# Two token groups through the norms of a two-layer transformer step: the last weight units are used twice, latent tokens first and context tokens second, and the layer loops are written out

## What is computed

```python
for l in range(2):
    h = rmsnorm(x, g[0]) * (1 + scale0) + shift0
    x = x + 0.5 * gate0 * rmsnorm(swiglu(h, wg[0], wu[0], wd[0]), g[1])   # 1024 -> 2816 -> 1024
    h = rmsnorm(x, g[2]) * (1 + scale1) + shift1
    x = x + gate1 * rmsnorm(mix(h @ w_in) @ w_out, g[3])    # Fourier | Hyena | attention
    h = rmsnorm(x, g[4]) * (1 + scale2) + shift2
    x = x + 0.5 * gate2 * rmsnorm(swiglu(h, wg[1], wu[1], wd[1]), g[5])
```

## Time and profile before

| | |
|---|---|
| median of 3 runs | 1707.72 us (1707.42 to 1708.83) |
| span of the profiled execution, first to last instruction | 1706.8 us |
| PE busy | 1607.5 us, 94% |
| PEld busy | 1462.8 us, 86% |
| DVE busy | 899.6 us, 53% |
| ACT busy | 765.5 us, 45% |
| mean granted PE clock | 0.985 of 2.4 GHz |
| moved by DMA | 268.20 MB, mean 157 GB/s |

### The profile page before, as it was taken

One profiled execution on the slowest core, in us unless ns is written; L12 is line 12 of the kernel. 1 busy time (PEld: TensorE's weight loads), 2 busy tenths in 40 slices (PEclk: granted clock), 3 DMA queues, 4 the chain that ended last, 5 costly groups with the idle time before them and its releaser, 6 DMA issues.

```text
span 1706.8 us, 26956 instructions
## 1 busy us (share of the span) xinstructions
PE 1607.5 (94%) x9434; PEld 1462.8 (86%) x9434; DVE 899.6 (53%) x1597; ACT 765.5 (45%) x1176; POOL 17.8 (1%) x39
## 2 busy tenths in 40 slices
PE   6799999998988899999989999999898889999996
PEld 2399989996966699989979998999696669998996
DVE  5655544336685655544336554533667565554433
ACT  2355544325535555543255544432552555554332
POOL 0000000000000000000000000000000000000000
PEclk9999999999999999999999999999999999999998
DMA  6833685345501433474343368534550144337331
GB/s 232 333 107 125 249 294 182 130 159 182 181 1 38 173 123 123 137 282 138 129 167 100 124 247 293 191 124 165 181 181 1 36 163 130 124 126 298 132 124 65
DMA packets 70613, 268.20 MB, mean 157 GB/s; under 512 B 9387, under 2 KB 10444, under 8 KB 69900
## 3 DMA queue, kind: packets, MB, share of 16 engines
q1 hardware_dynamic: 67164, 248.96, 41.7%
q0 software_dynamic: 3376, 18.35, 2.8%
HBM read 260.73 MB, written 6.55 MB: 157 GB/s over the span
## 4 chain that ended last, share of the span: by engine, by line
PE 87%; DVE 6%; issue 3%; DMA 2%; ACT 2%; POOL 0%; DVEq 0%; SPq 0%; ACTq 0%; POOLq 0%
PE bank L529 26%; PE bank L531 25%; PE bank L530 25%; PE bank L538 4%; PE bank L867 1%; PE bank L829 1%; DVE y L1271 1%; DMA w_m<-w_mod 1%; DVE rstd L1266 1%; PE bank L753 1%; PE bank L617 1%; DMA f_cst<-tneg 1%; DVE sb_s L1457 1%; ACT prob_t L1068 1%; PE bank L856 1%
## 5 line engine op out<-in xcount | busy, mean ns | idle before, releaser
L1207 DVE TENSOR_TENSOR w_lo<-w_raw,w_hi 128x1024 fp32r<-128x1024 f32 (+2 forms) x288 | 373.6, 1297 | 527.5 <-ACT w_hi L927 526.6
L529 PE MATMUL bank<-h_hi,w_hi 128*128 128x386 f32 (+1 forms) x1760 | 606.3, 344 | 1.3 <-DVE w_lo L1207 0.8
L531 PE MATMUL bank<-h_hi,w_lo 128*128 128x386 f32 (+1 forms) x1760 | 596.1, 339 | 0.0
L530 PE MATMUL bank<-h_lo,w_hi 128*128 128x386 f32 (+1 forms) x1760 | 595.5, 338 | 0.0
L927 ACT ACTIVATE w_hi<-w_raw 128x1024 fp32r<-128x1024 f32 (+2 forms) x288 | 322.1, 1118 | 528.2 <-PE bank L531 527.6
L529 PEld LDWEIGHTS bank<-h_hi,w_hi 128*128 128x128 f32 x1760 | 332.0, 189 | 20.9 <-issue 14.0
L530 PEld LDWEIGHTS bank<-h_lo,w_hi 128*128 128x128 f32 x1760 | 332.8, 189 | 1.2
L531 PEld LDWEIGHTS bank<-h_hi,w_lo 128*128 128x128 f32 x1760 | 332.3, 189 | 0.0
L530 PE MATMUL bank<-hid_lo,w_hi 128*128 128x384 f32 x704 | 238.4, 339 | 0.0
L529 PE MATMUL bank<-hid_hi,w_hi 128*128 128x384 f32 x704 | 238.4, 339 | 0.0
L531 PE MATMUL bank<-hid_hi,w_lo 128*128 128x384 f32 x704 | 238.4, 339 | 0.0
(11 more groups left out here) (194 smaller groups left out, 1123.5 us busy)
## 6 DMA issues: line engine op xcount, KB each, us to landing
w_raw<-w_gu SPq DMA_DIRECT2D x176, 512.0 KB, 3.3
w_m<-w_mod SPq DMA_DIRECT2D x160, 512.0 KB, 6.3
w_raw<-w_dn SPq DMA_DIRECT2D x64, 704.0 KB, 4.0
w_raw<-w_in SPq DMA_DIRECT2D x26, 512.0 KB, 3.4
w_raw<-w_out SPq DMA_DIRECT2D x16, 512.0 KB, 3.4
cst<-consts POOLq DMA_DIRECT2D x8, 688.0 KB, 5.9
spec<-f_spec POOLq DMA_DIRECT2D x2, 2304.0 KB, 8.2
spc<-spec POOLq DMA_DIRECT2D x8, 576.0 KB, 5.1
```

The source lines that it names most:

```text
L529: mm(out, w_hi[:, wn, c], rhs_hi, start=first, stop=False)
L530: mm(out, w_hi[:, wn, c], rhs_lo, start=False, stop=False)
L531: return mm(out, w_lo[s][:, c], rhs_hi, start=False, stop=last)
L1207: TT(w_lo[unit % RAW][:, 0:n], w_raw[unit % RAW][:, 0:n], w_hi[:, unit % HIS, 0:n], ALU.subtract).then_inc(unit_lo.sem, 1)
```

## The change

Three things.

1. *Two passes over the last units of each block.* `TAIL = (2, 4, 2)` output tiles, four weight units each time, stay in the ring: PE multiplies them first with the 256 latent columns, for all tiles, then again with the 128 context columns. The latent statistics are put inside the context pass. The first four units of the next block are also used in two passes, 258 latent columns and then 128 context columns. Statistics, root, reciprocal, `y`, `x`, squares, `h_hi` and `h_lo` are made for each group apart.
2. *Orders and buffers.* `HIS = 4`; conversion of the next units is put between the chunks of the norm and, in the loops, two units further ahead; a dummy square root loads ACT's table ahead of the norm; squares of a norm are added up in `xsq` by DVE before PE sees them (2 instead of 4 or 8 calls); the second four row tiles come after the first products of units 0 and 1; `z`, `vg_tok` and `prob_t` move to the memory of `w_m`.
3. *Layers written out*, and the two unread jobs of the last layer left out (`jobs_of`).

The core of the diff (the twins on ACT and DVE follow the same order; parts left out are marked):

```diff
-HIS = 2
+HIS = 4
+GROUP = (slice(NCTX, T), slice(0, NCTX))
+GROUP_H = (slice(NCTX, TB), slice(0, NCTX))
+TAIL = (2, 4, 2)
+TAIL_BANKS = {2: (1, 3), 4: (0, 2, 1, 3)}
...
+        def jobs_of(layer, n):
+            return 0 if n and layer == DEPTH - 1 else JOBS[n]
...
+            def first_units(layer, n, base, banks, post):
+                landed = layer * (32 * JL) + (JOB_NORM[n] * 32 + 64)
+                def part(u, g, ks):
+                    for k in ks:
+                        pe.wait_ge(nlo_done.sem, nlo_done.at(layer, 16 * n + 8 * g + k + 1))
+                        last = three(bank[banks[u]][:, GROUP_H[g]], (base + u) % RAW, (base + u) % HIS, k,
+                                     h_hi[:, k, GROUP_H[g]], h_lo[:, k, GROUP_H[g]], k == 0, k == KT - 1)
+                    if g and ks[-1] == KT - 1:
+                        last.then_inc(units_done.sem, 1)
...
+                job_rows(landed, range(MSLOT))
...
+                lo(0)
+                part(0, 0, (0, 1))
...
+                lo(1)
+                part(1, 0, (0, 1))
+                job_rows(landed, range(MSLOT, KT))
+                for u in range(2):
+                    part(u, 0, (2, 3))
+                if post:
+                    post_stats(*post, 1)
+                for u in range(2):
+                    part(u, 0, (4, 5))
+                lo(2)
+                part(2, 0, range(4))
+                for u in range(2):
+                    part(u, 0, (6, 7))
+                lo(3)
+                part(3, 0, range(4))
+                pre_stats(layer, n, 0)
+                for u in (2, 3):
+                    part(u, 0, range(4, KT))
+                part(0, 1, range(KT))
+                pre_stats(layer, n, 1)
+                for u in range(1, 4):
+                    part(u, 1, range(KT))
+            def tail(layer, n, unit, per_tile, hi, lo):
+                tiles = range(KT - TAIL[n], KT)
+                each = FT // 2 if per_tile == 2 else KT
+                for g, cols in enumerate(GROUP):
+                    for j, t in enumerate(tiles):
...
+                            for k in range(each):
+                                f = p * each + k
+                                last = three(bank[to][:, cols], u % RAW, u % HIS, k, hi[:, f, cols], lo[:, f, cols],
+                                             f == 0, f == per_tile * each - 1)
+                                if g and j == 0 and p == 0 and k == each - 3:
+                                    post_stats(layer, n, 0)
+                            if g:
+                                last.then_inc(units_done.sem, 1)
...
-                with pe.Fori(0, KT // 2) as i:
+                with pe.Fori(0, (KT - TAIL[2 * n]) // 2) as i:
...
-            with pe.Fori(0, DEPTH) as layer:
+            for layer in range(DEPTH):
...
+            def norm(post, pre, base=0):           # ACT
...
+                for g, cols in enumerate(GROUP):
...
+                    for c in range(4):
...
+                            A(xsq[:, (0, 1, 2, 1)[c], :, cols], x[:, 2 * c:2 * c + 2, cols],
+                              ACT.Square).then_inc(xsq_done.sem, 1)
+                            for k in (2 * c, 2 * c + 1):
+                                A(h_hi[:, k, cols], x[:, k, cols], ACT.Copy,
+                                  scale=coef_a[:, k, 1 - g:2 - g]).then_inc(nhi_done.sem, 1)
+                            if not g:
+                                hi_part(layer, base + c)
...
+            def norm(ch, post, pre, base=0):       # DVE
...
+                        if pre and c:
+                            input_lo(*pre, g, c - 1)
+                            if not g:
+                                lo_part(pre[0], base + c - 1)
```

More of the change, by code:

```diff
@@ L443, in ffn @@
                     gate_up(i)
[L444 to L447, removed]
+                if first < ROUNDS - 1:
+                    gate_up(first, own=True)
+                    with sp.Fori(first + 1, ROUNDS - 1) as i:
+                        gate_up(i, before=True, own=True)
+                gate_up(ROUNDS - 1, before=first < ROUNDS - 1)
                 with sp.Fori(0, KT // 2) as i:
@@ L494, in _ @@
                 pool.sem_inc(spec_free.sem, 1)
-            with pool.Fori(0, DEPTH) as layer:
-                pool.wait_ge(x_new.sem, x_new.at(layer, 4))
+            for layer in range(DEPTH):
+                pool.wait_ge(x_new.sem, x_new.at(layer, 8))
                 pool.sem_inc(pool_stage.sem, 1)
@@ L606, in _, with pre_stats @@
             pe.wait_ge(mod_ready.sem, 2)
-            def pre_norm(layer, n, tiles=None):
-                landed = layer * (32 * JL) + (JOB_NORM[n] * 32 + 64)
+            def pre_stats(layer, n, g):
+                pe.wait_ge(xsq_added.sem, xsq_added.at(layer, 6 * n + 3 * g + 3))
+                for k in range(2):
+                    last = mm(bank[STAT_PRE[g]][:, GROUP[g]], ones[:, :], xsq[:, 0, k, GROUP[g]], start=k == 0,
+                              stop=k == 1)
+                last.then_inc(pre_stat.sem, 1)
@@ L612, in pre_norm @@
                 pe.wait_ge(mod_copied.sem, mod_copied.at(layer, JOB_NORM[n]))
                 job_rows(landed, range(MSLOT))
[L614 to L650, removed]
+                if post:
+                    pe.wait_ge(out_taken.sem, out_taken.at(post[0], out_at(post[1], KT - TAIL[post[1]], 1) + 1))
@@ L655, in norm_job_turn @@
                 job_turn(layer * JL + (JOB_NORM[n] + 3))
[L657 to L664, removed]
             def ffn(layer, n):
-                first = ROUNDS - 1 - JOBS[n]
+                first = ROUNDS - 1 - jobs_of(layer, n)
                 def body(i, job, units=range(4)):
@@ L731, in tile_of @@
                     last.then_inc(units_done.sem, 1)
[L732 to L735, removed]
+                pe.wait_ge(in_copied.sem, in_copied.at(layer, 0))
+                first_units(layer, 1, B_IN, (0, 1, 2, 3), (layer, 0))
                 with pe.Fori(1, 3) as i:
@@ L871, in project_out @@
             def project_out(layer):
[L872 to L884, removed]
-            with pe.Fori(0, DEPTH) as layer:
+                for u in range(OUTT - TAIL[1]):
+                    unit = B_OUT + u
+                    pe.wait_ge(out_taken.sem, out_taken.at(layer, out_at(1, u) - 1))
+                    pe.wait_ge(unit_lo.sem, unit_lo.at(layer, unit + 1))
+                    for k in range(KT):
+                        if u == 0 and k == 4:
+                            pe.wait_ge(cat_lo.sem, cat_lo.at(layer, 8))
+                        last = three(bank[DOWN[u % 2]][:, 0:T], unit % RAW, unit % HIS, k, h_hi[:, k, 0:T],
+                                     h_lo[:, k, 0:T], k == 0, k == KT - 1)
+                    last.then_inc(units_done.sem, 1)
+                tail(layer, 1, B_OUT, 1, h_hi, h_lo)
+            for layer in range(DEPTH):
                 ffn(layer, 0)
@@ L927, in hi_part @@
                 A(w_hi[:, unit % HIS, 0:n], w_raw[unit % RAW][:, 0:n], ACT.Copy).then_inc(unit_hi.sem, 1)
[L929 to L946, removed]
-                        last.then_inc(nhi_done.sem, 1)
-                if not n:
-                    hi_part(layer, 1)
-                act.wait_ge(xsq_used.sem, xsq_used.at(layer, 4 * n + 4))
-                A(sd[:, :], bank[STAT][:, 0:T], ACT.Sqrt, bias=epsc[:, :]).then_inc(pre_sd.sem, 1)
@@ L968, in ffn, with sqrt_table @@
+            def sqrt_table():
+                A(sd[:, 0:1], epsc[:, :], ACT.Sqrt)
             def ffn(layer, n):
@@ L1247, in input_lo @@
                 for k in (2 * c, 2 * c + 1):
-                    dve.wait_ge(nhi_done.sem, nhi_done.at(layer, KT * n + k + 1))
-                    if k == 0:
+                    dve.wait_ge(nhi_done.sem, nhi_done.at(layer, 16 * n + 8 * g + k + 1))
+                    if k == 0 and g == 0:
                         TT(h_lo[:, :, T:TB], coef_b[:, :, :], h_hi[:, :, T:TB], ALU.subtract)
-                    for s, cols in enumerate((CTX, LAT)):
-                        last = STT(out=h_lo[:, k, cols], in0=x[:, k, cols], scalar=coef_a[:, k, s:s + 1],
-                                   in1=h_hi[:, k, cols], op0=ALU.mult, op1=ALU.subtract)
@@ L1286, in tile_steps @@
                     unit, tile = B_GU[n] + 4 * base + 2 * half, FT * n + 2 * base + half
-                    lo_part(layer, unit + 2, r)
                     if job and half:
@@ L1316, in tile_steps @@
                        ALU.subtract).then_inc(hid_lo_done.sem, 1)
+                    lo_part(layer, unit + 5, r)
                 with dve.Fori(0, first) as i:
@@ L1512, in _ @@
                 dve.sem_inc(vec_copied.sem, 1)
-                lo_part(layer, 0)
-                for c in range(4):
-                    input_lo(layer, 0, c)
-                lo_part(layer, 1)
-                pre_rstd(ch, layer, 0)
+                norm(ch, (layer - 1, 2) if layer else None, (layer, 0))
                 ffn(ch, layer, 0)
+                norm(ch, (layer, 0), (layer, 1), B_IN)
```

(3 more changed lines are left out.)

334 lines of the change are left out of this document (203 added, 131 removed).

## The result

The changed kernel takes 1735.82 us (median of 4 runs, 1734.67 to 1738.0); the kernel before, beside it, 1707.57 us (1706.72 to 1708.83). The ratio is 1.0164, 95% interval 1.015 to 1.0179: 28 us slower.

A forecast was written before the change was run, and what follows sets the result against it. PE, busy 94% of the span, was taken as the bound. Split pairs and late row tiles outweighed hidden norm stalls and left-out jobs: place sums gave +22.7 us, 1730 against 1707.7; own range 1712 to 1752, over the cases 1698 to 1755.

The forecast's parts named there:

- The pair: Split products in tails and first units: 0.232 us against 0.177 for one; 1296 pairs, 71 us more PE work.
- the left-out jobs: Last layer's unread jobs: four groups of 32 row matmuls at 1.86 us come off the chain, -7.4 us.
- The row tiles: Second four row tiles of w_m land late; PE loses 4.7 us at each of five boundaries, bounds 0 and 6.
- The places: Start +5.2 us; boundaries 1 to 5: +5.7, +4.3, +3.3, +6.2, +4.3; last norm +1.1.
- the fourth rival: Clock falls while PE waits for row tiles, slowing dense products behind: 3.4 us at five places, 1747 us; chance 11%.
- The last norm: Stretch at the last norm, with its tail products: 39.5 us before, 40.6 after, +1.1.
- At nothing: HIS = 4, conversions further ahead, table load and moved buffers count zero, hidden by ACT and DVE idle time.
- Loads that hide: Rival: weight loads hide, so a pair costs no more than 0.177 us; 1660 us in all; chance 12%.
- plain f32 rates for narrow products: Rival: narrow fp32r product runs as two records of 0.111 us, 144 us more, 1874 us; chance 7%.
- That the rows land in time: Rival: no wait for row tiles at the boundaries, 5 x 4.7 us less, 1706 us; chance 10%.
- The signs: PE busy up some 60 us to about 97%; job_rows wait at each boundary; wrong if first and third boundaries shrink.

The follow-up runs named there:

- split_258_128: The kernel before, with the products of the up units in the gate and up loops made in two passes, 258 then 128 columns; 1821.67 us.
- late_rows: The changed kernel with one line moved: job_rows for the second four row tiles comes after the latent statistics; 1706.15 us, ratio to before 0.9983.
- plain_table: plain_jobs plus a dummy square root on ACT ahead of the last tiles of each ffn and of project_out; 1690.64 us, ratio to before 0.9896.
- plain_jobs: The kernel before with only the layer loops written out and the last layer's two unread modulation jobs left out; 1697.08 us, ratio 0.9933.

## Why the prediction was right

**The forecast was 1730, measured 1735.82, with the mechanism it named**: pairs whose narrow part costs no less than a load, and a wait for row tiles in the place of the wait for the norm.

- *The pair.* Forecast 0.121 + 0.111 = 0.232 us, measured 0.120 + 0.111, and 0.232 by the time of split_258_128. 1296 of them are 71 us, where PE's busy time grew by 1658.5 - 1607.5 = 51; 7.4 of the missing 20 are the left-out jobs and 17 the statistics (their groups are busy 40.0 us before and 22.9 after). That is some 4 us more than is missing, which I didn't split further.
- *The row tiles.* Forecast: the last lands 9.5 us after the rows began, PE is through at 9.95, 4.7 us lost. In the timeline after, the rows begin at 398.95, the last group starts at 408.40 (9.45) and products follow at 409.41 (10.5). Lost: 5.2 us; the half microsecond over the forecast is the clock, at which the last eight row matmuls take 1.01 us instead of 0.45. late_rows takes this away, and its five boundaries give back 23.3 us where 5 x 4.7 = 23.5 stood. That the sum is so near is luck in part: the places differ (5.7, 4.2, 4.7, 6.1, 2.6), and at the second and fifth a wait for DVE of 1.6 us, which the forecast didn't have, takes part of the place of the one for the rows.
- *The places.* Forecast +5.2 (start), +5.7, +4.3, +3.3, +6.2, +4.3, +1.1 (last), jobs -7.4. The windows of after, set against the same stretches of before (30.9, 58.5, 51.6, 60.9, 58.0, 51.6, 39.5), with the 0.2 us taken off: +6.8, +6.8, +6.3, +3.3, +7.6, +4.9, and -0.1 for the last, 35.6 in all. Of the span's difference of 26.2, the other -9.4 lie outside these places: 0.9 ahead of the first norm (73.34 against 72.42), and 8.5 in the loops, where the four job groups were forecast at 7.4. So the places cost 5.5 us more than the 30.1 forecast, and 2.0 us that I hadn't counted on came back elsewhere.
- *The rest*, 3.5 us of span (26.2 against 22.7), is what these leave, and the fourth rival is in it. The clock did fall during the waits, as it said (0.94 to 0.97 in the windows of after, 1.00 at the boundaries of late_rows). Behind the waits the products at 1.2 GHz cost 0.3 to 1.3 us a boundary over their 0.120 (3 to 14 distances of 0.20 us or more), against the 3.4 us of the rival; the other part of the half-clock time lay under the waits themselves and in the row matmuls. The start shows it best. The rows are through at 86.31, 13.9 us after its beginning as forecast, but the 16 distances of products from there to 89.92 take 3.61 us instead of 1.92: 1.7 us, and the start cost 1.6 over its forecast (6.8 against 5.2). Moving the rows doesn't cure that: late_rows has 23 distances of 0.20 us or more there, behind waits for `w_lo`.
- *The last norm* I had 1.2 us too dear.
- *At nothing.* That the table load counts for nothing in the changed kernel is not shown, as no run takes it out there. In the unsplit kernel it isn't hidden: taken away alone it was worth 6.4 us (plain_table). The prediction passed over that 18 us were to be had there and in the jobs, without the split.
- *Rivals.* Loads that hide, and plain f32 rates for narrow products, fall by the measured distances (0.111 and 0.120). The Trainium skill's gap of N/2.4 + 2.5 ns ("TensorE: Matmul & The Clock Gate", Back-to-back issue gap), which that section gives for matmuls without their loads, would make 56 and 110 ns of the pair; the runs give 111 and 120, and even at 64 columns 111. The floor is the size that its section on LDWEIGHTS gives for the load (P/1.2, 107 ns for 128). That the rows land in time falls by the five pieces on the chain. That this rival's 1706 is what late_rows measured, 1706.15, is luck in part: 4.2 us of its gain came from the start and 1.7 from the mixers, and the changed kernel had been 6 us over its own forecast.
- *The signs.* PE busy rose by 51 us to 96%, where some 60 and 97% were named; the wait at `job_rows` came at each boundary; the first and third boundaries grew.

Where the gain went, worked out from the traces of plain_table and late_rows: PE's idle time fell from 93.7 us (1690.2 - 1596.5) to 60.0, so 34 us of stalls went. PE's busy time grew by 48 us, as 71 us of pairs came, 17 of statistics went, and some 6 us more went that fit less work at half clock (mean clock 0.986 and 0.994). 48 - 34 is the 14 us between the spans, and the medians say 15.5. In the changed kernel itself, the rows in the middle of the latent products cost another 29.7 us.

## What to carry to other kernels

Before a pass is split along the moving dimension, count the weight loads: no piece here, however narrow, cost less than 0.11 us, the distance of two loads. So the split pays only where the stalls that it covers are larger than the number of pairs times what a pair costs more; here 71 us of pairs against 34 us of stalls and some 23 us of other PE work saved. A step that is moved earlier takes its DMAs' slots with it, so look at what has to land before it in the new place: one call moved behind the latent products gave back 29.7 us. And when a change is a bundle, time its cheap parts alone: those here won 18 us, while the bundle lost 28.

## What the runs showed of the hardware that was not expected

- An fp32r product that loads its own 128x128 weights takes 0.111 us at 64, 128 and 192 columns, 0.120 at 258, 0.147 at 322 and 0.177 at 386: flat up to somewhere between 194 and 258, then with the columns, 57 ns for the last 128. At 386 that is 0.016 us above one column per cycle at 2.4 GHz, and at 258 0.0125.
- The clock after short waits: in the kernel after, with waits of 1.74, 1.06, 0.59 and 0.33 us between groups of row matmuls, it fell to 1.2 GHz within them, and behind them 258-column products start 0.21 to 0.22 instead of 0.12 us apart for five distances; in late_rows, without those waits, the granted clock of all five boundaries is 1.00.
- The load of the root's table takes 1.28 us of ACT (plain_jobs, 386.47), of which 0.92 showed in when the root starts.
